# GpSimd's low-part subtraction: pieces of 256 columns or one instruction per part

## The reference

```python
qkv = einsum('bsd,de->bse', x, w_qkv)                 # 1024 x 3072
s = einsum('bqhcd,bkhcd->bhcqk', q_blk, k)            # 8 heads, 2 maps each
p = softmax(where(mask, s, NEG_INF)); a = p[:, :, 0] - lam * p[:, :, 1]
o = rms_norm(einsum('bhqk,bkhe->bqhe', a, v), g_sub) @ w_o
h = layer_norm(ALPHA * h + o)
h = layer_norm(ALPHA * h + (silu(h @ w_gate) * (h @ w_up)) @ w_down)   # width 2816, twice
proj = h @ w_in                                       # mLSTM and stick-breaking heads
act = gelu(einsum('cd,ced->ce', xb, u[eb])) * gb      # experts: in, gate
y = einsum('ce,ced->cd', act, v[eb])                  # experts: out
```

## Time and profile before

| | |
|---|---|
| median of 3 runs | 1750.41 us |
| profiled execution, its own time | 1752.44 us |
| its span in the profile | 1750.9 us |
| PE busy | 1677.0 us, 96% |
| DVE busy | 1049.7 us, 60% |
| ACT busy | 851.9 us, 49% |
| POOL busy | 622.5 us, 36% |
| mean granted TensorE clock | 0.986 of full speed |
| longest chain of waits | PE 84%, DVE 6%, ACT 4%, POOL 3% |

### The profile page before, as it was taken

One profiled execution on the slowest core, in us unless ns is written; L12 is line 12 of the kernel. 1 busy time (PEld: TensorE's weight loads), 2 busy tenths in 40 slices (PEclk: granted clock), 3 DMA queues, 4 the chain that ended last, 5 costly groups with the idle time before them and its releaser, 6 DMA issues.

```text
span 1750.9 us, 29515 instructions
## 1 busy us (share of the span) xinstructions
PE 1677.0 (96%) x11486; PEld 1530.0 (87%) x11486; DVE 1049.7 (60%) x1769; ACT 851.9 (49%) x1254; POOL 622.5 (36%) x783
## 2 busy tenths in 40 slices
PE   7989999999999999987999989999999999999997
PEld 5778999899899988865989989999999888888886
DVE  5565555366555544564134577899878555555555
ACT  5566444344544445654443444454455454555553
POOL 0667100050500025433651454657654422222221
PEclk9999999999999999998999999999999999999999
DMA  8334555555555545332334566666555677777775
GB/s 320 129 136 148 195 190 176 209 193 180 199 190 180 193 167 196 129 122 95 110 136 166 172 210 212 196 211 188 177 193 185 203 248 242 241 240 241 241 241 175
DMA packets 98073, 331.70 MB, mean 189 GB/s; under 512 B 10972, under 2 KB 44284, under 8 KB 79376
## 3 DMA queue, kind: packets, MB, share of 16 engines
q1 hardware_dynamic: 95904, 322.94, 54.9%
q0 software_dynamic: 2032, 6.89, 1.2%
HBM read 310.91 MB, written 18.87 MB: 188 GB/s over the span
## 4 chain that ended last, share of the span: by engine, by line
PE 84%; DVE 6%; ACT 4%; POOL 3%; issue 2%; DMA 2%; SPq 0%; DVEq 0%; ACTq 0%; POOLq 0%
PE banks L978 20%; PE banks L467 12%; PE banks L415 8%; PE banks L417 8%; PE banks L416 8%; PE banks L943 6%; PE banks L945 6%; PE banks L944 6%; PE banks L439 3%; POOL uL L2305 3%; PE banks L932 2%; PE banks L404 1%; DVE wL L1536 1%; ACT wH L1003 1%; DMA raw<-in_qkv 1%
## 5 line engine op out<-in xcount | busy, mean ns | idle before, releaser
L2268 POOL TENSOR_TENSOR wL<-raw,wH 128x256 fp32r<-128x256 f32 x376 | 280.9, 784 | 573.1 <-ACT wH L1003 572.9
L2059 DVE TENSOR_TENSOR uL<-raw,uH 128x1024 fp32r<-128x1024 f32 x192 | 241.2, 1256 | 227.4 <-ACT uH L1463 227.1
L1463 ACT ACTIVATE uH<-raw 128x1024 fp32r<-128x1024 f32 x256 | 270.1, 1056 | 166.5 <-PE banks L978 166.4
L415 PE MATMUL banks<-xH,wH 128*128 128x256 f32 x1216 | 343.3, 282 | 7.6 <-DVE xL L1563 7.6
L416 PE MATMUL banks<-xL,wH 128*128 128x256 f32 x1216 | 342.2, 281 | 0.0
L417 PE MATMUL banks<-xH,wL 128*128 128x256 f32 x1216 | 342.2, 281 | 0.0
L2305 POOL TENSOR_TENSOR uL<-raw,uH 128x256 fp32r<-128x256 f32 x256 | 234.1, 945 | 238.7 <-ACT uH L1463 238.7
L1536 DVE TENSOR_TENSOR wL<-raw,wH 128x2048 fp32r<-128x2048 f32 (+1 forms) x95 | 216.9, 2284 | 157.7 <-ACT wH L1003 157.5
L1003 ACT ACTIVATE wH<-raw 128x2048 fp32r<-128x2048 f32 (+1 forms) x154 | 269.9, 1762 | 79.6 <-PE banks L467 67.7
L943 PE MATMUL banks<-xH,uH 128*128 128x256 f32 x1024 | 297.3, 290 | 9.5 <-POOL uL L2305 9.2
L944 PE MATMUL banks<-xL,uH 128*128 128x256 f32 x1024 | 290.4, 284 | 0.0
(11 more groups left out here) (318 smaller groups left out, 2677.0 us busy)
## 6 DMA issues: line engine op xcount, KB each, us to landing
raw<-in_eu SPq DMA_DIRECT2D x128, 512.0 KB, 4.2
raw<-in_ev SPq DMA_DIRECT2D x128, 512.0 KB, 3.4
raw<-in_gu SPq DMA_DIRECT2D x44, 1024.0 KB, 4.8
raw<-in_dn SPq DMA_DIRECT2D x22, 1024.0 KB, 4.8
gelu_scratch<-st SPq DMA_DIRECT2D x128, 128.0 KB, 3.9
st<-gelu_scratch SPq DMA_DIRECT2D x128, 128.0 KB, 3.3
raw<-in_win SPq DMA_DIRECT2D x14, 1024.0 KB, 5.5
raw<-in_qkv SPq DMA_DIRECT2D x12, 1024.0 KB, 7.1
```

The costliest lines, as they stand in the source:

```text
L415: e.matmul(o, wh[:, w0:w0 + P], H[:, k, :], start=k == 0, stop=False)
L1463: e.activation(uH[n % US][:, :], raw[k // 2][:, (k % 2) * UW:(k % 2) * UW + UW], ACT.Copy).then_inc(s_uh, 1)
L2059: e.tensor_tensor(uL[n % US][:, :], raw[k // 2][:, (k % 2) * UW:(k % 2) * UW + UW], uH[n % US][:, :].bitcast(F32), ALU.subtract).then_inc( ...
L2268: r = e.tensor_tensor(wL[n % NS][:, d], raw[n % NR][:, d], wH[n % NS][:, d].bitcast(F32), ALU.subtract)
```

## The change

The constant `PW` and both inner loops go. POOL issues one instruction per part (2048 or 1024 columns) and one per expert block (1024 columns). The waits, the counts, the order of the parts and the data are the same.

```diff
@@ gpsimd, split
                     c = part_cols(n, p)
                     e.wait_ge(s_hi, HI[n] + p + 1)
-                    for c0 in range(c.start, c.stop, PW):
-                        d = slice(c0, c0 + PW)
-                        r = e.tensor_tensor(wL[n % NS][:, d], raw[n % NR][:, d], wH[n % NS][:, d].bitcast(F32), ALU.subtract)
-                    r.then_inc(s_log, 1)
+                    e.tensor_tensor(wL[n % NS][:, c], raw[n % NR][:, c], wH[n % NS][:, c].bitcast(F32), ALU.subtract).then_inc(s_log, 1)
@@ gpsimd, usplit
             e.wait_ge(s_uh, n + 1)
-            for c0 in range(0, UW, PW):
-                d = slice(c0, c0 + PW)
-                r = e.tensor_tensor(uL[n % US][:, d], raw[k // 2][:, (k % 2) * UW + c0:(k % 2) * UW + c0 + PW], uH[n % US][:, d].bitcast(F32), ALU.subtract)
-            r.then_inc(s_ulg, 1)
+            e.tensor_tensor(uL[n % US][:, :], raw[k // 2][:, (k % 2) * UW:(k % 2) * UW + UW], uH[n % US][:, :].bitcast(F32), ALU.subtract).then_inc(s_ulg, 1)
```

More of the change, by code:

```diff
@@ L34 @@
 PAUSE = 2
-PW = 256
 BASE = 16512
```

## The result

The changed kernel took 1764.49 us (median of four executions, 1761.64 to 1765.71), the kernel before 1750.18 in the same comparison. The ratio is 1.0077, 95% interval 1.0059 to 1.0094: slower by 10 to 16 us. I had forecast 1754.2 us, in a range up to 1763. The direction was right, the size was not. A later comparison, with 12 executions against 35, gave 1.0043 (1.0027 to 1.0060), 1763.41 against 1755.28 us.

What follows compares the result with a forecast made beforehand. PE, busy 96% of the span, was taken as the bound, so POOL counts only through PE's waits. Losses of 11.9 less gains of 8.1 gave +3.8 on 1750.41: 1754.2 us, own range 1750 to 1761, wider range 1743 to 1763.

Steps and rivals of the forecast that it cites:

- The instruction's length: One whole POOL instruction takes 2.44 us for 1024 columns and 4.76 for 2048, from 0.58 per piece plus 0.12 once.
- The layers: DVE instructions that meet a whole POOL part wait for its rest; the places on PE's path lose 11.9 us in sum.
- Og: Memory keys, 95 us: parts of 1024 hold DVE's scaling, Am and Og; PE starts their transposes 4.6 us later.
- oL: wo parts at 121.67 and 139.34 us hold the scaling, Am and oL: losses of 1.7 and 1.0 us.
- Stick-breaking: At 705.97 us POOL gets in after line 1826 and holds line 1827, which PE needs: loss 2.0 us.
- mLSTM: End of the mLSTM, 800.08 us: POOL holds line 1881 and so the products of line 1903: loss 1.6 us.
- The others: Rotary products, layer norms and convolutions go both ways: together +1.0 us, between -1 and +3, a guess.
- The experts: Expert stage wins 8.1 us: 1.3 at the first block, 3.3 at 1036.09, 2.1 in five other waits, 1.4 from the clock.
- DVE keeps its turn: Rival, chance 0.22: DVE goes first at changes of turn, layer losses fall to 4.7 us; -6.2 us, 1744 us.
- nothing saved: Rival, chance 0.13: whole instructions save nothing, 2.8 and 5.6 us; +11.6 us, 1762 us.
- wrong: Refuting signs: Og's wait below 6, a part over 5.3 us, or new PE waits for DVE's odd blocks or line 932.
- The clock: From 1043.0 to 1046.4 us the granted clock is 0.50; with a shorter wait it stays at full speed, gaining 1.4 us.

Runs made afterwards that it cites:

- the kernel with that half alone: Against the kernel before: one POOL instruction per part for the layers' weights only, expert blocks kept in pieces of 256; 1764.25 against 1755.28 us, ratio 1.0062.
- the expert half alone: Against the kernel before: one POOL instruction per even expert block only, weights kept in pieces of 256; 1751.76 against 1755.28 us, ratio 0.9979.
- the repeat: The changed kernel run once more, nothing altered, against the kernel before; 1763.41 against 1755.28 us, ratio 1.0043.

## Why the prediction failed

**The instruction's length.** Right: 2.39 and 4.57 us against 2.44 and 4.76. The 4.497 us that the Trainium skill gives for 2048 columns ("GPSIMD Engine Reference", Elementwise — side-by-side cycle accounting) was the nearer value; the trace has 4.566. The 5.56 us for eight pieces in my working is a row at 43.9 us that I did not show; the rows named have 5.66 to 5.82.

**The layers, forecast 11.9 us.** Measured 7.3 of PE's idle, and +9.0 of time in the kernel with that half alone. Place by place, as the shift of PE's instructions between the two profiles (forecast in brackets):
- Og: 3.3 (4.6), by PE's wait for it. DVE's scaling, `Am` and the first Og product were each held by one part in turn (2.28, 2.33 and 2.42 us), so POOL and DVE alternate strictly:

```profile
93.87 9.43 POOL L2265 TENSOR_TENSOR wL<-raw,wH 128x1024 fp32r<-128x1024 f32 x4 [5.72 <-ACT wH L1002]
```

```profile
96.45 2.28 DVE L1663 TENSOR_SCALAR Sm<-Sm,sm 128x128 f32<-128x128 f32 x1
98.77 2.33 DVE L1668 SCALAR_TENSOR_TENSOR Am<-Sm,sm 128x128 f32<-128x128 f32 x1
```

  I had let Og wait for the fourth part and counted 0.35 us of POOL's time for each DVE instruction between; POOL's four parts took 9.43 us without any such loss, and started 1.1 us earlier.
- oL: 1.4 (1.7) and 1.4 (1.0), the second in two steps, of which the first (0.7) is a longer wait for Og at 142.
- Stick-breaking: 0 (2.0). Line 1827 (1826 after) was held about as forecast (5.62 us), but PE does not wait for it. I took the operand of PE's line 711 for `zs`; the row said `ze`, which line 1826 had finished. `zs` is read by DVE itself, at 720.3 us, 2.4 after it was ready. The group of line 1826 after, and PE's timeline:

```profile
L1826 DVE TENSOR_TENSOR zs<-zs,cst x2: 1219/3420/5621, 712.3 to 743.4; 128x1024 f32<-128x1024 f32 x2
```

```profile
716.30 0.81 PE L710 MATMUL banks<-ze,cst 128*128 128x384 f32 x2
```

- mLSTM: 2.1 at the first wait behind the hold, 1.4 after the next (1.6). It was a single value per row that was held:

```profile
810.63 2.74 DVE L1880 SCALAR_TENSOR_TENSOR dn<-dn 128x1 f32<-128x1 f32 x1
```

- The others, a guess of 1.0: the one at 778 cost 1.1 (5.1 to 6.2 for eL), the one at 50 gave 0.7. One that I had excluded was there: "PE does not wait" for the layer weights was wrong, PE waited 3.1 us for POOL's `wL` near 660 before and 0.7 after; but its wait for xL at 669 grew from 1.4 to 3.9 and took this back.

**The experts, forecast -8.1 us.** This is the step that failed: "DVE in this stage: a block costs it up to 2.32 us at once instead of four times 0.58, the same total, and POOL is blocked less often; I count it at nothing". POOL was blocked less often, but once for 9.3 us, and DVE's own blocks came late. The listed gains came: the first block 1.4 (1.3), 1043 us 3.4 (3.3), the five small waits all went, and the stretch of slow clock at 1043 was gone. Against them stand two new waits, 2.1 us at 1057 for DVE's odd block, which stood behind a product (line 2149) that a whole POOL block had stretched from 2.28 to 4.48 us, and 6.8 at 1193, with a slow clock behind it. Without the clock term I had summed 6.7 us of idle saved; with the expert half alone it grew by 1.1. The mechanism that ran is that of my rival "DVE keeps its turn", but in the other stage: in the layers POOL got in (Og's wait was 7.1 us, not below 6), and on the expert blocks DVE kept its turn, which hurts. I had priced that rival as a gain only. The rival nearest in the number, "nothing saved" at 1762, is refuted by the lengths, 2.39 and 4.57 us and not 2.8 and 5.6. The signal that I had named under "wrong", new waits in this stage for odd blocks, was there, and a worse one that I had not named: POOL's even block kept out by DVE. The earlier trace rows gave the hint, pieces of up to 2.77 us, and I used them for a chance and not for a term. A plainer one stands in the kernel before on the expert blocks' own line, which I did not show: a piece of 3.70 us, passed over at eight starts of DVE from 1241.2 on.

```profile
L2305 POOL TENSOR_TENSOR uL<-raw,uH x256: 715/742/3696, 948.2 to 1380.3; 128x256 fp32r<-128x256 f32 x128
```

**The clock, forecast -1.4.** In the profiled pair PE's busy time does fall by 1.4, but that is luck. In the repeat it rises by 5.0, at a granted clock of 0.980, and the four timed executions of the first comparison have 0.981 to 0.983 where the kernel before was profiled at 0.986. In the repeat's comparison the mean is 0.982 against 0.984, worth up to 4.4 us (an estimate: 0.0025 of 1755). I had counted the one stretch that would go, at 1043, and none that new waits bring, as behind 669 and 1193. How much of the distance between the +6.8 of the first profile and the +14.3 of the medians the clock explains is not settled; the repeat gave +8.1.

Sum without the clock: forecast 11.9 - 6.7 = +5.2 us of idle, measured +8.2 and +7.6. That this is off by only 2 to 3 us is luck: the layers lost 4.6 us less than forecast (11.9 against 7.3), and the experts missed their term by 7.8 (6.7 saved against 1.1 lost).

## What to carry to other kernels

When two engines shut each other out, count chains and not instructions: from where an engine arrives, run down the other's list to its next gap or to an instruction that needs no lock, and take that distance as the long end of the wait and the rest of one instruction as the short end. The runs here have both, and which of them comes is not predicted. Cutting pieces smaller can make the hold longer. An instruction that needs no lock, put into the chain, let POOL in within the trace; that it is worth its place in time is not shown beyond whole blocks alone. And read the operand's name in the row of the waiting instruction before a held instruction is put on the path.

## What the hardware showed

- Beside POOL's f32 subtraction these DVE instructions were held until it ended: two-input ones from SBUF down to 128x1 (2.74 us), also with one input, TENSOR_SCALAR 128x128 f32 to f32 (2.28 for 0.28) and CAST uint32 to f32 (2.31 for 0.21). Not held: MAX8, FIND_INDEX8, MATCH_REPLACE8, TENSOR_REDUCE, RECIPROCAL 128x2, TENSOR_SCALAR 128x1, and subtractions with one input in PSUM (0.68 for 128x512); beside POOL they kept their usual length, as MAX8 with 0.27 us and FIND_INDEX8 with 0.41 over 256 columns. The Trainium skill, "SBUF — State Buffer", Who interferes with whom, says that the shared pair of ports is held for a whole instruction, which the rows bear out.
- Who goes next differs. In the layers of the changed kernel no whole part took more than 5.62 us where 4.57 is usual, so POOL waited 1.1 us at the most; in the experts' gapless chains it was passed over at 13 boundaries in a row (1188.5 to 1197.1), and with POOL's pieces of 128 one DVE product waited behind 19 of them (8.05 us). Why one boundary lets the other in and the next does not stays open.
- POOL's fixed cost is small: 0.742 us for 256 columns, 1.297 for 512, 2.39 for 1024, 4.57 for 2048. As an estimate from these, one instruction more costs about 0.2 us (2 x 1.297 - 2.39), and in a row, where the pieces overlap, 0.16 (eight in 5.66 us, less 4.57, by seven).
